# Keys at the upper end of SBUF, with W_out and the first feed-forward weights loaded ahead of their stages

## The reference

```python
for l in range(DEPTH):                                     # 2
    px = project(modulate(rms_norm(x, g_pre_mix[l]), mx[0], mx[1]), w_in[l], gq_a[l], gk_a[l], rope)
    ...                                                    # the context tokens likewise
    mix_x = token_mix(px, k_a, v_a, k_c, v_c, ...)         # attention, gated mixing, then  y @ w_out
    x = x + mx[2] * rms_norm(mix_x, g_post_mix[l])
    ...
    fx = conv_ffn(modulate(rms_norm(x, g_pre_ffn[l]), mx[3], mx[4]), w_up[l], w_conv[l], b_conv[l], w_down[l])
    x = x + mx[5] * rms_norm(fx, g_post_ffn[l])
```

## Time and profile before

| | |
|---|---|
| median of 3 runs | 3644.01 us (3639.72 to 3644.27) |
| the profiled execution | 3643.01 us, span 3641.2 us |
| PE busy | 3273.6 us (90%) |
| DVE, ACT, POOL busy | 55%, 34%, 21% |
| mean granted clock of TensorE | 0.957 |
| seam attention to output projection | near 889 us and 2716 us |
| seam output projection to feed-forward | near 1045 us and 2849 us |

### The profile page before, as it was taken

One profiled execution on the slowest core, in us unless ns is written; L12 is line 12 of the kernel. 1 busy time (PEld: TensorE's weight loads), 2 busy tenths in 40 slices (PEclk: granted clock), 3 DMA queues, 4 the chain that ended last, 5 costly groups with the idle time before them and its releaser, 6 DMA issues. The chain is left out here.

```text
span 3641.2 us, 47510 instructions
## 1 busy us (share of the span) xinstructions
PE 3273.6 (90%) x17608; PEld 2603.8 (72%) x17608; DVE 1987.3 (55%) x2736; ACT 1238.5 (34%) x1865; POOL 765.0 (21%) x900
## 2 busy tenths in 40 slices
PE   5988769997979999999997698899979799999996
PEld 3877247775868888888885587677758677777775
DVE  3755347775544445444546565677755444444445
ACT  3432246664432122212112442566644321221221
POOL 1333235553110000000003343455530100000003
PEclk8999889998989999999999898899989899999998
DMA  6542930002311111111103553100013211111113
GB/s 222 185 154 91 400 120 26 26 32 98 122 64 46 40 35 39 41 40 35 35 29 114 183 201 137 47 20 32 32 62 140 68 48 46 47 46 45 50 36 116
DMA packets 194214, 304.82 MB, mean 84 GB/s; under 512 B 22250, under 2 KB 144114, under 8 KB 182834
## 3 DMA queue, kind: packets, MB, share of 16 engines
q1 hardware_dynamic: 191985, 302.51, 23.9%
q10 hardware_dynamic: 2113, 0.77, 0.1%
HBM read 235.06 MB, written 68.19 MB: 83 GB/s over the span
## 5 line engine op out<-in xcount | busy, mean ns | idle before, releaser
L2154 DVE TENSOR_TENSOR ff_acc<-ff_dn,ff_acc 128x512 f32<-128x512 f32 x396 | 271.5, 688 | 329.9 <-PE ff_dn L122 329.5
L2037 POOL TENSOR_TENSOR ff_ms<-ff_ss,c_eps 128x1 f32<-128x1 f32 x18 | 16.8, 935 | 1662.9 <-ACT ff_t_gate L2117 1662.9
L120 PE MATMUL ff_z_gate<-h_hT,ff_u_hi 128*128 128x512 f32 (+1 forms) x880 | 329.6, 375 | 27.2 <-DVE ff_u_lo L2129 27.2
L120 PE MATMUL ff_dn<-ff_d_lo,ff_a_hi 128*128 128x512 f32 x792 | 320.2, 404 | 34.7 <-issue 17.0
L122 PE MATMUL ff_z_gate<-h_hT,ff_u_hi 128*128 128x512 f32 (+1 forms) x880 | 328.1, 373 | 0.0
L121 PE MATMUL ff_z_gate<-h_hT,ff_u_lo 128*128 128x512 f32 (+1 forms) x880 | 327.6, 372 | 0.0
L120 PE MATMUL ff_z_value<-h_hT,ff_u_hi 128*128 128x512 f32 (+1 forms) x880 | 327.3, 372 | 0.0
L122 PE MATMUL ff_z_value<-h_hT,ff_u_hi 128*128 128x512 f32 (+1 forms) x880 | 326.5, 371 | 0.0
L121 PE MATMUL ff_z_value<-h_hT,ff_u_lo 128*128 128x512 f32 (+1 forms) x880 | 325.9, 370 | 0.0
L2140 DVE SCALAR_TENSOR_TENSOR ff_t_gate<-ff_z_gate,c_vec,ff_t_gate 128x1023 f32<-128x1023 f32 (+1 forms) x132 | 132.1, 1014 | 348.9 <-ACT ff_t_gate L2092 342.1
L121 PE MATMUL ff_dn<-ff_d_hi,ff_a_lo 128*128 128x512 f32 x792 | 311.1, 393 | 0.0
(11 more groups left out here) (282 smaller groups left out, 7426.8 us busy)
## 6 DMA issues: line engine op xcount, KB each, us to landing
ff_u_raw<-in_w_up_dram SPq DMA_DIRECT2D x88, 512.0 KB, 3.8
ac_m_wm<-in_w_mod_dram SPq DMA_DIRECT2D x40, 1024.0 KB, 8.8
ff_d_raw<-in_w_down_dram SPq DMA_DIRECT2D x44, 512.0 KB, 4.4
hT_d<-fr_hs SPq DMA_DIRECT2D x20, 1024.0 KB, 5.1
kv_hs<-hT_d SPq DMA_DIRECT2D x20, 1024.0 KB, 4.8
q_d<-fr_qs SPq DMA_DIRECT2D x18, 512.0 KB, 2.7
q_d<-fr_qs SPq DMA_DIRECT2D x36, 256.0 KB, 3.0
mo_y<-y_d SPq DMA_DIRECT2D x18, 512.0 KB, 4.5
```

Of the source, the lines that this page charges most:

```text
L120: e.matmul(out, w[0], x[1], start=start, stop=False)
L2154: e.tensor_tensor(out, dn[:, half, :], out, ALU.add).then_inc(acc_done, 1)
```

## The change

The keys and values get a fixed place at SBUF's upper end (`KEYS_AT`). W_out's tiles (`OutLoads`) and those of slice 0 of W_up (`UpLoads`) get fixed places inside that region, so that they outlive a phase. Three things then move.

- The four DMAs of W_out are issued in the attention phase "al", as soon as the last scores (its last readers of the keys) are made. The output phase issues none.
- The two DMAs of slice 0 of W_up are issued in the output phase, once its last projection is done (it lies in the place of W_out's lo part).
- Slice 0 is split in the output phase: ACT's two casts (`split_hi`) behind `norm(N - 1)`, DVE's two subtractions (`split_lo`) ahead of the two `lo(N - 1, h)`. The feed-forward phase starts with its semaphores preset.

```diff
@@ attention_phase, SP
+            if next_load:
+                e.wait_ge(sA_done, STEPS * blocks)
+                e.wait_ge(sC_done, STEPS * blocks)
+                next_load(e)
             for u in range(2):
                 store(blocks - 1, u)
@@ new classes (cut)
+class OutLoads:
+    ...
+    def first(self, e):
+        for i in range(KD // 2):
+            e.dma_start(self.raw[:, 2 * i:2 * i + 2, :], self.w_v[:, 2 * i:2 * i + 2, :]).then_inc(self.loaded[i], 16)
+class UpLoads:
+    ...
+    def split_hi(self, e, s):
+        e.wait_ge(self.loaded[s], 16)
+        e.copy(self.hi[:, s], self.raw[:, s]).then_inc(self.hi_done, 1)
+    def split_lo(self, e, s):
+        e.wait_ge(self.hi_done, s + 1)
+        e.tensor_tensor(self.lo[:, s], self.raw[:, s], self.hi[:, s], ALU.subtract)
@@ mix_out_phase, SP
             load_y(0)
-            for i in range(KD // 2):
-                e.dma_start(w_raw[:, 2 * i:2 * i + 2, :], w_v[:, 2 * i:2 * i + 2, :]).then_inc(w_in[i], 16)
             load_y(1)
@@
+                if i == N:
+                    e.wait_ge(mm_done, N)
+                    up.first(e)
                 if i >= 1:
                     store(i - 1)
@@ mix_out_phase, ACT
                 if 0 <= i - 1 < N:
                     norm(i - 1)
+                if i == N:
+                    for s in range(2):
+                        up.split_hi(e, s)
@@ mix_out_phase, DVE
+                for h in range(2):
+                    if h and i + 1 < N:
+                        y_lo(i + 1, 1)
+                    if 0 <= i - LAG < N:
+                        modulate(i - LAG, h)
+                        if i - LAG == N - 1:
+                            up.split_lo(e, h)
+                        lo(i - LAG, h)
@@ ffn_phase, SP, ACT, DVE
-            load_up(0, 0)
-            load_up(0, 1)
...
-            split_up(0, 0)
-            split_up(0, 1)
+            e.sem_inc(u_hi_done, 2)
...
-            e.sem_inc(u_lo_done, 2)
+            e.sem_inc(u_lo_done, 4)
```

More of the change, by code:

```diff
@@ L68 @@
 V_N = V_BS + BG
+KEYS_AT = 152416
+WO_AT = 160000
+U_AT = 161696
 def rope_tables():
@@ L1065, in kv_phase @@
         h_in, rope_in_s = [ph.sem("h_in0"), ph.sem("h_in1")], ph.sem("rope_in")
+        assert ph.next_place() <= KEYS_AT
         mm_done = ph.sem("mm_done")
@@ L1220, in _, with attention_phase @@
                 post_k(r)
-def attention_phase(nc, l, c, name, b0, blocks, n_keys, q_d, y_d, stage, late_of=None):
+def attention_phase(nc, l, c, name, b0, blocks, n_keys, q_d, y_d, stage, late_of=None, next_load=None):
     NK = n_keys * P
@@ L1710, in gates, with mix_out_phase @@
     return sync, vector
-def mix_out_phase(nc, l, c, t0, inp, mod_d, y_d, x_of, xs_d, hT):
+def mix_out_phase(nc, l, c, t0, inp, mod_d, y_d, x_of, xs_d, hT, wo, up):
     N, LAG = NT - t0, 2
     with Phase(nc, f"mo{l}") as ph:
-        w_raw, w_lo = ph.pair("w_raw", "w_lo", [P, KD, D])
-        w_hi = ph.sb("w_hi", [P, KD, D], F32R)
+        w_raw, w_hi, w_lo, w_in = wo.raw, wo.hi, wo.lo, wo.loaded
         hf = ph.sb("hf", [P, KD, P])
@@ L1727, in mix_out_phase @@
         y_in, x_in, x_stored = ([ph.sem(f"{m}{u}") for u in range(2)] for m in ("y_in", "x_in", "x_stored"))
-        w_in = [ph.sem(f"w_in{i}") for i in range(KD // 2)]
+        assert ph.next_place() <= WO_AT
         w_hi_done, w_lo_done = ph.sem("w_hi_done"), ph.sem("w_lo_done")
@@ L1956, in ffn_phase @@
         acc = ph.sb("acc", [P, n, D])
+        tz = [ph.sb("t_gate", [P, TOKS]), ph.sb("t_value", [P, TOKS])]
+        d_raw = ph.sb("d_raw", [P, D])
+        if ph.next_place() < U_AT:
+            ph.sb("gap", [P, (U_AT - ph.next_place()) // 4])
+        assert ph.next_place() == U_AT
+        u_raw, u_hi, u_lo = up_first.raw, up_first.hi, up_first.lo
+        ph.sb("u_place", [P, 3, 2, KD, P])
         ss, ms, rs = (ph.sb(m, [P, n]) for m in ("ss", "ms", "rs"))
@@ L2083, in split_up @@
             def split_up(j, s):
-                e.wait_ge(u_in[s], j * 16 + 16)
+                e.wait_ge(u_in[s], j * 16)
                 e.wait_ge(up_done, j * 2 + (s + 1))
@@ L2219, in hybrid_block_kernel @@
     with Phase(nc, "c") as ph:
+        loads = ph
         shared = Consts()
@@ L2249, in hybrid_block_kernel @@
                 with Phase(nc, f"keys{l}") as keys:
-                    c.kA = keys.sb("kA", [P, 4, TOK], F32R)
-                    c.kC = keys.sb("kC", [P, 2 * CH, TOK], F32R)
-                    c.v = keys.sb("v", [P, NT, AKV + CH, HD])
+                    at = keys.within((KEYS_AT, 4 * (4 * TOK + 2 * CH * TOK + NT * (AKV + CH) * HD)))
+                    c.kA, c.kC = at("kA", [P, 4, TOK], F32R), at("kC", [P, 2 * CH, TOK], F32R)
+                    c.v = at("v", [P, NT, AKV + CH, HD])
+                    wo, up = OutLoads(nc, loads, l, inp), UpLoads(nc, loads, l, inp)
                     kv_phase(nc, l, c, kl, hT_d, inp["rope"])
```

37 lines of the change are left out of this document (19 added, 18 removed).

## The result

| | before | changed |
|---|---|---|
| median | 3642.03 us (3639.72 to 3644.27, 4 runs) | 3612.11 us (3611.82 to 3612.89, 4 runs) |
| ratio | | 0.9920, interval 0.9908 to 0.9931 |
| span of the profiled execution | 3641.2 us | 3611.1 us |
| mean granted clock | 0.957 | 0.959 |

The changed kernel is 29.9 us faster. The forecast was 18 us, 3626, with a range down to 3619; it started from a median of 3644.0, which a fourth run has since brought to 3642.0. The direction was right; the time lies outside the range.

What follows compares the result with a forecast made beforehand. PE works 90% of the span, so only its standstill or lower clock could be gained. Terms 2.7 + 5.0 + 4.8 + 5.4 = 17.9 us off 3643.01 gave 3625.1, stated as a median of 3626.0, range 3619 to 3635.

Steps and rivals of the forecast that it cites:

- The moved keys and tiles cost nothing: Step of the sum, whole kernel: new places of keys and tiles add 0 us, since no instruction changes its shape.
- W_out's start, 2.7 and 5.0: Seam attention to output projection: W_out loaded in the attention's tail ends DVE's `w_lo` chain 2.7 and 5.0 us earlier by layer.
- the first rival: PE stays at the lower clock through the output phase's first pass: 3.7 us less gained, 3630; chance 0.15.
- the 873 that I worked out: Attention's tail: W_out's 4.19 MB at 399 GB/s take 10.5 us and land near 873, 16 us ahead of the barrier.
- W_up's start, 4.8 and 5.4: Seam to the feed-forward stage: with slice 0 loaded and split earlier, PE starts 4.8 and 5.4 us sooner by layer.
- The tail: End of the output phase: the added casts and subtractions make it end 2.1 us later.
- PE's wait: Start of the feed-forward stage: PE's wait of 27.2 us in two times should read some 17.
- The second rival: Something the old wait hid holds PE at the feed-forward start, 3 us more per layer: 3632; chance 0.10.
- The fill of `acc`: Feed-forward start: the 8.63 us fill ends 9.7 us into the stage, hidden because DVE needs it at least 15 us in.
- That the phases' end doesn't move: Rival: loads move but another engine's wait takes each place, so the time is some 3639; chance 0.06.
- That stores queue behind W_out and make the kernel slower: Rival: y's stores wait behind W_out in SP's one queue; at 14 us a layer 3653; chance 0.03.

Runs made afterwards that it cites:

- e4_places_only: The changed kernel's places of all tiles with the old order of W_out's loads and of slice 0 of W_up; 3626.21 us, ratio 0.9958.
- e5_pad512: The kernel before, with pads ahead of the feed-forward tiles that make W_up's operand distance a multiple of 512 bytes; 3625.73 us, ratio 0.9956.
- e9_hT_moved: The changed kernel with hT and u both 96 bytes further in the first layer, hT alone 128 bytes in the second; 3624.92 us, ratio 0.9950.
- e8_aligned: The changed kernel with W_out, keys and the front's hs also brought to operand distances that are multiples of 512 bytes; 3604.81 us, ratio 0.9894.

## Why the prediction was right on the seams and wrong in the sum

**The step that failed** is "The moved keys and tiles cost nothing: no instruction changes its shape." The shapes are the same, but the pace of a matmul also goes by how far apart its two operands lie, and the change alters that distance in three stages: W_up, W_out and the scores. That step should have carried 17.9 us of gain in the W_up products, some 3.5 us of loss in W_out's and up to 2 in the scores (an estimate from 1.6 ns on each of their products). `e4_places_only` shows the sum of it apart from the order (16 us), `e5_pad512` shows it without any of the new places (17 us), and `e9_hT_moved` shows what in the places it is. The trace before held the hint: the same matmul, `ff_z_value` with 512 columns, at 229.1 ns in one layer and 234.3 in the other. I never compared the two layers.

**W_out's start, 2.7 and 5.0.** The mechanism was right: W_out issued 0.1 us behind the last score, the chain of seven unchanged at 8.03 us, the gates' product directly behind it. In the changed kernel the stretches gave 0.81 and 3.58, since 480 and 384 output products lost 4.2 ns each. With the pace taken out, the first layer's 2.7 is borne out (2.4 to 2.6). The second layer's 5.0 was too large: 3.4 to 3.9 against three other executions of the old order, because the one trace that I read has a later start of the chain than the other three. That `e8_aligned` gives 5.10 against that same trace is luck in part. The lower clock did not eat the gain, so the first rival did not happen: the granted clock rose from 0.50 to 1.00 at 903.6 and 2722.9, 8.3 and 9.1 us behind the first transposes, where I had worked out 8. W_out landed by about 875.4 (last issue near 864.1, longest 11.3 us), 2 us later than the 873 that I worked out from 399 GB/s, with 14 us still to spare.

**W_up's start, 4.8 and 5.4.** 4.43 and 5.25. The tail grew by 1.85 us in both layers (2.1 forecast). PE started 1.75 and 1.49 behind DVE's last `lo` instead of 1.1: it needs 0.5 to 0.7 us more than POOL behind the same barrier, which no row of before showed. PE's wait is 17.5 us, "some 17" forecast. The second rival, PE held 3 us more, is out. The fill of `acc` ends at 1057.33 and DVE's first tap starts at 1067.07, so it is hidden in the first layer as worked out.

**The rivals.** That the phases' end doesn't move: no. That stores queue behind W_out and make the kernel slower: half of it happened. The first of the last block's stores went out at 833.81 before and took 2.0 us to land; now it goes out at 864.73, right behind W_out, and takes 11.4, and the next two take 3.3 instead of 1.7 and 1.8. Nobody waits for them: the last store takes 1.8 us as before, and the time from last score to first transpose of y is 32.69 us against 32.41 before, 31.71 against 31.62 in the second layer.

**The range** was made of the spreads of clock, barrier and median alone. It had no room for a term that I had set to exactly nothing without a row for it.

## What to carry to other kernels

When tiles move in SBUF, treat it as a change of every matmul that reads them: read the start-to-start step of each matmul form, by stage and layer, before and after, and compare it between stages that should be alike. Here 7 ns a step over 2112 matmuls outweighed both seams. For these fp32r products of 512 columns the place to aim at is a distance between stationary and moving operand that is a multiple of 256 bytes, and a pad of 80 to 104 floats buys it here. For 256 columns it is no gain (W_up and the front's products were some 2 ns slower there). Judge small seam edits by the stretch that they act on, since whole runs here spread by several us, and read a seam in more than one execution: the start of the `w_lo` chain in the second layer varied by 2.4 us in the old order.

## What the runs showed of the hardware that I had not expected

- The step of a matmul depends on the distance of its two operands, stationary less moving, modulo 256 bytes. With W_up: 226.7 ns at 0, 229.0 at 192, 233.2 at 32, 64 and 128, 234.3 at 96. W_out and the front's products give the same figures to 0.5 ns at 32, 96 and 192, and to 2 at 0. At 32, 64 and 128 the steps alternate (229 and 237 ns one after the other at 128), at 0 nearly all are 226 or 227.
- At distance 0 the median step is 227 ns for W_up, W_down, W_out, keys and the front alike. The higher means of some stages come from the product behind each group of transposes, which takes some 315 ns to the next start.
- Open is why W_out takes 230.5 in the first layer of `e9_hT_moved`, at a distance of 0 with other places. Nor do the runs say why a distance matters; that the two reads meet in the same memory would be a guess.
- Behind a barrier PE started 0.74 and 0.49 us later than POOL, with nothing left to wait for.
